# Grouped attention: the causal mask as an identity product on the tensor engine instead of an addition on VectorE

## The reference

```
s_s = einsum(q_b, k_g) * scale ; p_s = masked_softmax(s_s, key_pos <= t)
s_w = einsum(q_b, k_b) * scale ; p_w = masked_softmax(s_w, (w_pos <= t) & (w_pos > t - WINDOW))
out = g[..., 0:1] * o_c + g[..., 1:2] * o_s + g[..., 2:3] * o_w
```

## Time and profile before

| | us |
|---|---|
| median of 3 runs | 3494.77 (3492.79 to 3507.03) |
| the profiled execution | 3506.3 |
| its span, first to last instruction | 3504.5 |
| the 32 steps and their end | 2653.0 to 2993.8 |

### The profile page before, as it was taken

How to read it: one execution, slowest core, us unless ns; L and a number is a source line. 1 busy time by engine, 2 the same in 40 slices (tenths; PEclk the granted TensorE clock), 3 DMA queues, 4 the chain that set the end, 5 groups by cost and what they waited for, 6 DMA issues and landing times. The chain is left out here.

```text
span 3504.5 us, 38396 instructions
## 1 busy us (share of the span) xinstructions
PE 3233.8 (92%) x14296; PEld 2455.8 (70%) x14296; DVE 1794.2 (51%) x2495; ACT 696.9 (20%) x1434; POOL 1592.6 (45%) x834
## 2 busy tenths in 40 slices
PE   6999879989999999987998999979899998699998
PEld 5888655467888788865545788857766765568886
DVE  4313596644324531349665432356455877555525
ACT  2101102331001110110234100123323444121101
POOL 4656540026666566654001665635423322046664
PEclk9999989999999999998999999989879998689999
DMA  3323311002323232332100232322211111113322
GB/s 120 108 84 104 109 62 39 1 29 86 114 79 105 81 112 80 105 109 66 39 1 25 84 111 83 106 79 90 86 37 61 55 43 37 51 61 108 97 82 75
DMA packets 65485, 263.13 MB, mean 75 GB/s; under 512 B 7390, under 2 KB 8606, under 8 KB 63808
## 3 DMA queue, kind: packets, MB, share of 16 engines
q1 hardware_dynamic: 61344, 238.86, 21.1%
q10 hardware_dynamic: 4000, 22.37, 1.7%
HBM read 259.10 MB, written 2.10 MB: 75 GB/s over the span
## 5 line engine op out<-in xcount | busy, mean ns | idle before, releaser
L472 POOL TENSOR_SCALAR w_hi<-w_raw 128x1024 fp32r<-128x1024 f32 (+2 forms) x415 | 471.0, 1135 | 1854.5 <-PE psum L506 1606.1
L474 POOL TENSOR_TENSOR w_lo<-w_raw,w_hi 128x1024 fp32r<-128x1024 f32 (+2 forms) x415 | 1121.5, 2702 | 34.7
L504 PE MATMUL psum<-u_hi,w_hi 128*128 128x512 f32 x2368 | 943.5, 398 | 36.9 <-DVE u_lo L1581 32.1
L505 PE MATMUL psum<-u_lo,w_hi 128*128 128x512 f32 x2368 | 930.9, 393 | 0.0
L506 PE MATMUL psum<-u_hi,w_lo 128*128 128x512 f32 x2368 | 929.3, 392 | 0.0
L504 PEld LDWEIGHTS psum<-u_hi,w_hi 128*128 128x128 f32 x2368 | 450.1, 190 | 162.5 <-issue 44.9
L506 PEld LDWEIGHTS psum<-u_hi,w_lo 128*128 128x128 f32 x2368 | 450.5, 190 | 95.7
L505 PEld LDWEIGHTS psum<-u_lo,w_hi 128*128 128x128 f32 x2368 | 450.9, 190 | 94.9 <-issue 3.9
L504 PE MATMUL psum<-h_hi,w_hi 128*128 128x512 f32 x960 | 374.4, 390 | 5.6 <-DVE h_lo L1706 5.2
L506 PE MATMUL psum<-h_hi,w_lo 128*128 128x512 f32 x960 | 373.6, 389 | 0.0
L505 PE MATMUL psum<-h_lo,w_hi 128*128 128x512 f32 x960 | 373.5, 389 | 0.0
(11 more groups left out here) (287 smaller groups left out, 3693.7 us busy)
## 6 DMA issues: line engine op xcount, KB each, us to landing
w_raw<-in_w SPq DMA_DIRECT2D x335, 512.0 KB, 3.5
w_raw<-in_w SPq DMA_DIRECT2D x48, 768.0 KB, 4.2
w_raw<-in_w SPq DMA_DIRECT2D x32, 640.0 KB, 3.8
dft<-in_dft ACTq DMA_DIRECT2D x2, 2048.0 KB, 12.2
idft<-in_idft ACTq DMA_DIRECT2D x2, 2048.0 KB, 7.8
w_c<-in_w_c ACTq DMA_DIRECT2D x2, 2048.0 KB
x<-in_xt SPq DMA_DIRECT2D x1, 2048.0 KB, 8.6
decay<-in_decay ACTq DMA_DIRECT2D x2, 1024.0 KB, 6.0
```

The costliest lines, as they stand in the source:

```text
L472: pool.tensor_scalar(hi, raw, 1.0, 1.0, ALU.mult, ALU.mult).then_inc(w_hi_ready, 1)
L474: pool.tensor_tensor(lo, raw, hi.bitcast(F32), ALU.subtract).then_inc(w_split, 1)
L504: pe.matmul(out, hi[:, c, :], rhs_hi(c), start=(s == 0), stop=False)
L505: pe.matmul(out, hi[:, c, :], rhs_lo(c), start=False, stop=False)
```

## The change

The four score matmuls of a step no longer close their accumulation. After them PE issues four more fp32 matmuls with the identity as weights and the 128 x 128 mask as moving operand, onto the last 128 columns of each of the four score tiles: first both branches of head 0, then both of head 1. The signal that head e's scores are complete moves from its second score matmul to its second identity product. DVE's addition of the mask goes, with the wait of the maximum for it.

```
-  mm = pe.matmul(score[e][:, b, 0:u["n"]], u["qk"][b][1], u["qk"][b][2], start=True,
-                 stop=True, skip_group_check=True)
-  if b == 1:
-      mm.then_inc(s_full, 1)
+  pe.matmul(score[e][:, b, 0:u["n"]], u["qk"][b][1], u["qk"][b][2], start=True,
+            stop=False, skip_group_check=True)
+  for e, (u, _) in enumerate(now):
+      for b in range(2):
+          mm = pe.matmul(score[e][:, b, u["n"] - P:u["n"]], ident[:, :], causal[:, :],
+                         start=False, stop=True, skip_group_check=True)
+      mm.then_inc(s_full, 1)
...
-  edge = sc[:, :, n - P:n]
   dve.wait_ge(s_full, k + 1)
-  link(dve.tensor_tensor(edge, edge, causal[:, :].unsqueeze(1).broadcast_to([P, 2, P]), ALU.add))
   link(dve.tensor_reduce(mx[:, j, 0:2], sc[:, :, 0:n], AX.X, ALU.max))
```

## The result

The changed kernel took 3524.05 us (median of 6, 3511.03 to 3526.57) against 3494.84 (median of 6, 3492.79 to 3507.03) for the kernel before: the ratio is 1.0069, 95% interval 1.0045 to 1.0093. Forecast were 3521 and a range of 3503 to 3545.

What follows compares the result with a forecast made beforehand. PE's ordered list was taken to bound the attention stage; 24.9 us of products plus 1.6 for half clock minus 0.4 gave 26.1, on the median 3494.8 thus 3521 us, range 3503 to 3545.

Steps and rivals of the forecast that it cites:

- What bounds the kernel: Attention stage: PE's ordered list sets each step with a projection (12.19, 11.83, 8.87 us); copies, maxima and exponentials set steps 19, 23, 27, 31.
- The price of a product: Each added fp32 identity product on PE costs 0.222 us, as line 990's do; four cost 0.89 us a step.
- The cheap rival: An identity product on PE costs what a transpose does, 0.11 us: 12.3 us in all, 3507 us, no change; chance 0.12.
- the dear one: Unhidden weight loads or the turn from half-row to full-row matmuls cost up to 1.6 us a step: 45 us, 3540; chance 0.09.
- Covered by slack of 1.27 us: In the step at 2721.70 scores end 1.27 us before DVE reaches the mask, which covers the 0.89 us signal delay.
- Removed in these steps the additions give nothing: In the 27 steps with a projection and step 28, DVE's mask additions stand on no path; removing them saves nothing.
- The sum: Whole stage: 28 steps at 0.89 us, 24.9; plus 1.6 for half clock, minus 0.4 for steps 19, 23, 27, 31: 26.1 us.
- Step 19: Step without a projection: ACT's wait for DVE becomes a wait for the copy; length changes by -0.1 us, near 11.4.
- The clock: Rival: more PE work in steps 19, 23, 27, 31 may hold 2.4 GHz, about 9 us back: 17 us, 3512; chance 0.07.
- The end of the stage: After the last step without a projection (31): the clock rival had some 4 us back there, the forecast 0.1.
- DVE's list is the pace: Rival: the softmax chain sets each step, so removing additions saves 13.5 us (3481), or 27.1 with both (3468); chance 0.04.

Runs made afterwards that it cites:

- the third session: The changed kernel without an edit, timed again against the kernel before: two runs at 3515.1 and 3516.0 us, four at 3524.2 to 3526.2; ratio 1.0052.

## Why the prediction was right, and where it was not

The time was inside the range and 3 us from the forecast, but partly by luck: 26.1 us were forecast for the change, it costs about 17.5, and the rest of the 29 us between the medians comes from how the runs fell on the two levels, which the prediction did not know of. It took the 11.5 us between the profiled run and the median as plain offset; the profiled run was on the upper level, the median on the lower.

- *What bounds the kernel*: right, but for the six i = 2 steps below. PE's list sets the other steps with a projection; removing DVE's addition left 17 of 18 untouched to 0.05 us.
- *The price of a product*: right, 0.222 us, taken from line 990 at the same type and clock and nearly the same size (124 columns). The cheap rival (0.11) fell with the 256 records, two to a product, and the steps' growth of 0.89; the dear one with that growth and the doubled products.
- *Covered by slack of 1.27 us*: right; after the change ACT waits for DVE's bias in no step with a projection but the first.
- *"Removed in these steps the additions give nothing"*: this is the step that failed, in six i = 2 steps. The sum gave them 0.89 each, 5.3 us; they paid 2.2. There DVE was late in the kernel before, and the pause it made on PE, some 0.5 us each, took in part of the added work. The addition was on that path (without it 0.53 less), yet the longer list closes the pause by itself (10.15 with the addition kept), so in the changed kernel the removal adds nothing to that. The evidence lay in views I used. The 1.4 us of rows 3 are four pauses, one in each of the i = 2 steps 6, 10, 14 and 18, and I called them set off by PE itself. The waits of ACT over the same stretch have this third row, in the kernel before:

```profile
ACT e L1235 <- PE psum L679: 2.2, 4, 0.6
```

It names PE for a wait that DVE ended, as the timeline of step 6 shows. Rows 4 show the same 2.2 us. I counted only rows that name DVE.

- *Step 19*: the order of events was right, the length was not: 11.00 us for about 11.4. The walk forecast that ACT's exponentials would start 0.06 us earlier; against the scores they start 5.08 us on instead of 5.19, and PE's copies are the later part. The step is shorter by 0.1 for that; 0.28 of the other 0.37 lie in the value products (2.55 against 2.83 us), which begin at the half clock in both and in the changed kernel no longer end there.
- *The clock*: the rival had a part of the truth, but how much of it the change brings is not shown. Step 23 of the changed kernel took 9.69 us in one execution and 11.35 in the other. The windows of that step, first the one, then the other:

```profile
2894.55:2904.24 9.69, 6.42 (x54) 4.15 (x52) 7.44 (x15) 5.14 (x15) 2.58 (x2) 1.00 0.16 56
```

```profile
2907.97:2919.32 11.35, 8.08 (x55) 5.49 (x53) 8.68 (x18) 5.15 (x15) 2.58 (x2) 0.78 0.14 48
```

The same program, 1.00 against 0.78 of the clock and 1.66 us. The prediction's row for the half clock in step 19 was one execution of it. The steps behind (20, 24, 28), for which I had added 0.9 in all on top of 0.89 each, paid 1.4 us together and not 3.6: that term was too large. In step 20 of the changed kernel the scores take 0.72 us and not 0.99, so the clock was back before them. The end of the stage gave back 1.7 us, where the rival had some 4 and the forecast 0.1; in the profile of the third session it gave back 0.1. With one trace of the kernel before, chance and the change cannot be told apart here.

- *DVE's list is the pace*: fell, as forecast; without the additions the stage was 3.9 us shorter and not 13.5.

## What to carry to other kernels

Work moved from an engine with slack to the one whose list sets the pace costs its full price there wherever that list has no pause, and the price is best taken from a row of the same operation, type and clock; here 128 products at 0.222 us forecast the lengthening of 18 steps to 0.2 us in 16. A mask of zeros and one large number needs no fp32: the same product in bf16 costs a quarter. Before the removal of an instruction is called worthless, look in the timeline for the instruction that ended just ahead of each short pause, whatever name the wait carries; and before a profile's time is set against a median, look whether their clocks agree outside the changed stage.

## What the runs showed of the hardware

- DVE's scaling of SBUF tiles is held up by POOL's elementwise pass over SBUF: two of 0.37 us take 3.30 together beside a pass of 2.39, and 0.73 with the pass cut to 16 columns.
- An fp32 product of 128 columns is two records of 0.111 us at 2.4 GHz, a bf16 one a single record of 0.05. Behind matmuls on half the rows the first four such fp32 products lengthened a step by 0.89 us, the next four by 0.88.
- The granted clock differs between executions of one program in stretches where PE pauses: 0.74 or 0.85 over the same 140 us, about 14 us in the whole time.
